# Pool projection moved into the attention loop, and the output projection's first chunk taken by feature blocks

## The reference, cut to what matters

```
def pool_mixer(u, w_pool, pool_scale):
    groups = jnp.split(u, N_POOL, axis=-1)            # 4 groups of 256 features
    outs = [(centred_mean(g, w) - g) @ w_pool[i] for i, (g, w) in enumerate(zip(groups, POOL_WINDOWS))]
    return jnp.concatenate(outs, axis=-1) * pool_scale

mix = jnp.concatenate([context_attention(q, k, v), pool_mixer(u, w_pool[l], pool_scale[l])], axis=-1) @ w_out[l]
yp = yp + m_ctx[2][:, None] * mix                      # the gate row
```

## Time and profile before

| what | value |
|---|---|
| median of 3 runs | 4318.09 us |
| the profiled execution's own time | 4316.63 us |
| its span, first to last instruction | 4315.0 us |
| PE busy | 3882.6 us, 90% |
| DVE, ACT, POOL busy | 2562.3 us, 1821.1 us, 507.7 us |
| mean granted TensorE clock | 0.948 |

### The profile page before, as it was taken

The page is one execution under the profiler, slowest core; times in us unless marked ns, Lnnn a source line. Parts: engine busy times, 40 slices in busy tenths (PEclk is TensorE's granted clock), DMA queues, the critical chain, the costliest instruction groups (busy, mean ns, idle before and its releaser), DMA issues. The chain is left out here.

```text
span 4315.0 us, 69324 instructions
## 1 busy us (share of the span) xinstructions
PE 3882.6 (90%) x25083; PEld 3405.9 (79%) x25083; DVE 2562.3 (59%) x4875; ACT 1821.1 (42%) x2862; POOL 507.7 (12%) x458
## 2 busy tenths in 40 slices
PE   7899999999799997595996299999999999999992
PEld 3688888888688895595995288888888888888881
DVE  4655554555567766231321767777777777777774
ACT  3511111110576663111113066666666666666663
POOL 0000000000444652000000000000000000000000
PEclk9999999999899998798998699999999999999996
DMA  9434434343544445635325167777777777777776
GB/s 350 139 127 134 133 130 137 127 134 116 136 137 113 119 136 195 222 103 176 112 80 190 54 225 253 255 257 258 258 255 255 254 253 254 255 256 254 253 241 251
DMA packets 568508, 818.44 MB, mean 190 GB/s; under 512 B 23600, under 2 KB 455296, under 8 KB 556544
## 3 DMA queue, kind: packets, MB, share of 16 engines
q1 hardware_dynamic: 545760, 699.64, 50.0%
q0 software_dynamic: 22688, 118.02, 8.5%
HBM read 715.89 MB, written 101.71 MB: 189 GB/s over the span
## 5 line engine op out<-in xcount | busy, mean ns | idle before, releaser
L1758 DVE TENSOR_TENSOR e_wlo<-e_raw,e_whi 128x1024 fp32r<-128x1024 f32 x768 | 905.0, 1219 | 355.5 <-ACT e_whi L1674 352.5
L1899 PE MATMUL ps<-e_xs,e_whi 128*128 128x320 f32 x4096 | 1061.4, 345 | 16.6 <-DVE e_xs L1766 9.0
L1899 PE MATMUL ps<-e_xs,e_wlo 128*128 128x160 f32 x4096 | 934.6, 238 | 0.0
L1674 ACT ACTIVATE e_whi<-e_raw 128x1024 fp32r<-128x1024 f32 x768 | 768.9, 1054 | 386.0 <-DMA e_raw<-in_w_gate 153.2
L1899 PEld LDWEIGHTS ps<-e_xs,e_whi 128*128 128x128 f32 x4096 | 754.8, 188 | 26.5 <-DVE e_wlo L1758 13.9
L1899 PEld LDWEIGHTS ps<-e_xs,e_wlo 128*128 128x128 f32 x4096 | 770.1, 191 | 0.7
L1302 PE MATMUL ps<-o_whi,mhi 128*128 128x256 f32 x1280 | 364.5, 285 | 101.2 <-DMA mlo<-mixlo 101.2
L1917 PE MATMUL ps<-e_whi,e_h 128*128 128x512 f32 x1024 | 405.4, 396 | 7.8 <-DVE e_h L1792 7.8
L484 PE MATMUL ps<-hhi,p_whi 128*128 128x512 f32 (+1 forms) x1536 | 386.6, 360 | 8.5 <-DVE p_wlo L423 8.5
L441 DVE SCALAR_TENSOR_TENSOR p_acc<-p_modraw,cT,p_acc 128x256 f32<-128x256 f32 x960 | 386.4, 478 | 0.6 <-DMA p_modraw<-in_w_mod 0.6
L484 PE MATMUL ps<-hlo,p_whi 128*128 128x512 f32 (+1 forms) x1536 | 383.5, 358 | 0.0
(11 more groups left out here) (237 smaller groups left out, 6037.7 us busy)
## 6 DMA issues: line engine op xcount, KB each, us to landing
e_raw<-in_w_gate SPq DMA_DIRECT2D x64, 2048.0 KB
e_raw<-in_w_up SPq DMA_DIRECT2D x64, 2048.0 KB
e_raw<-in_w_down SPq DMA_DIRECT2D x64, 2048.0 KB
p_modraw<-in_w_mod SPq DMA_DIRECT2D x128, 512.0 KB, 3.7
m_raw<-in_w_mod SPq DMA_DIRECT2D x16, 2048.0 KB, 14.6
p_raw<-in_w_in SPq DMA_DIRECT2D x64, 512.0 KB, 4.8
o_raw<-in_w_out SPq DMA_DIRECT2D x16, 2048.0 KB, 8.8
projT<-p_out_st POOLq DMA_DIRECT2D x32, 640.0 KB, 3.6
```

The lines of the kernel that those rows point to most:

```text
L1674: nc.scalar.activation(piece(whi, c, q), piece(raw, c, q), ACT.Copy).then_inc(w_hi_made, 1)
L1758: nc.vector.tensor_tensor(piece(wlo, c, q), piece(raw, c, q), piece(whi, c, q).bitcast(F32), ALU.subtract).then_inc(w_lo_made, 1)
L1899: last = nc.tensor.matmul(bank[:, 0:cols], w[:, s, at:at + P], xs[:, k, 0:cols], start=(k == 0 and w is whi), stop=(k == KD - 1 and w is whi))
```

## The change

In the attention stage:

- `mean_d` is twice as tall and POOL stores each mean block twice, so that output block n finds its pair of input blocks in 256 rows of its own. `w_pool` is copied by 8 DMAs inside DRAM to `wp_d`, laid out by output block.
- In bodies 2 to 7 PE does the projection of block n = j - 2: two fp32 matmuls after `values(5)`, two after `values(7)` and two (of 256 columns) after `values(9)`, all in bank 7. ACT (`pool_high`) reads PSUM, scales and rounds to hi; DVE (`pool_low`) makes lo from PSUM in one operation. Blocks 6 and 7 follow after the loop, one after the other.
- SP at a body's end stores block j - 2 and loads mean, weights and scale of block j - 1.
- The loop over j is written as a loop over 0 and 1 and one over 2 to 7.

In the output projection:

- The first block is gone. The gate rows are made at the start of the second one, in banks 5 to 7.
- SP loads the first weight chunk, then the four quarters of the mix, then the second weight chunk. Each quarter has its own semaphore.
- The first chunk of each half is taken `by_rows`: k outermost, the five tiles inside, in five banks; PE waits for the quarter k // 4 alone. All other chunks go `by_tiles` as before.

So block 7's inputs are asked for only once block 6 is projected and split; block 6's inputs are the last loads of the loop. The core of the diff:

```diff
+            def project_pool(n, t):
+                t0, tn = THIRDS[t]
+                if t == 0:
+                    pe.wait_ge(pool_in, n * 48 + 48)
+                if t:
+                    pe.wait_ge(pooled_lo, n * 3 + (t + AHEAD))
+                for b in range(2):
+                    last = nc.tensor.matmul(pool_bank(t)[:, 0:tn], wpn[:, b, :], mean[:, b, t0:t0 + tn],
+                                            start=(b == 0), stop=(b == 1))
+                last.then_inc(pooled, 1)
...
+            def pool_high(n, t):
+                t0, tn = THIRDS[t]
+                act.wait_ge(pooled, n * 3 + (t + 1))
+                if t == 0:
+                    act.wait_ge(pooled_stored, n * 32 + AHEAD)
+                nc.scalar.activation(plhi[:, t0:t0 + tn], pool_bank(t)[:, 0:tn], ACT.Copy, scale=pscn[:, 0:1]
+                                     ).then_inc(pooled_hi, 1)
...
+            def pool_low(n, t):
+                t0, tn = THIRDS[t]
+                dve.wait_ge(pooled_hi, n * 3 + (t + 1))
+                nc.vector.scalar_tensor_tensor(out=pllo[:, t0:t0 + tn], in0=pool_bank(t)[:, 0:tn], scalar=pscn[:, 0:1],
+                                               in1=plhi[:, t0:t0 + tn].bitcast(F32), op0=ALU.mult, op1=ALU.subtract
+                                               ).then_inc(pooled_lo, 1)
...
+            with pe.Fori(0, 2) as j:
+                body(j, False)
+            with pe.Fori(2, J) as j:
+                body(j, True)
+            pe.wait_ge(batch_read, J * NB + (NB - 1))
+            for n in (NPOOL - 2, NPOOL - 1):
+                for t in range(3):
+                    project_pool(n, t)
...
                 with sp.Fori(0, 2) as g:
                     sp.wait_ge(tile_done, g * (NCH * TPG) + 2 * TPG)
+                    load_w(g, 0, 0)
                     for q in range(4):
                         for dst, src in ((mhi, mixhi_d), (mlo, mixlo_d)):
                             sp.dma_start(dst[:, 4 * q:4 * q + 4, :].bitcast(F32),
                                          src[q * 512:q * 512 + 512, ds(g * GT, GT)].rearrange("(k p) t -> p k t", p=P)
-                                         ).then_inc(mix_in, 16)
-                        if q < 2:
-                            load_w(g, q, q)
+                                         ).then_inc(mix_in[q], 16)
+                    load_w(g, 1, 1)
...
+                def by_rows(g, i, s):
+
+                    for k in range(KD):
+                        if k % 4 == 0:
+                            pe.wait_ge(mix_in[k // 4], g * 32 + 32)
+                            piece_there(g, i, s, k // 4)
+                        for t in range(TPG):
+                            if k == 0:
+                                free_bank(g, i, s, t)
+                            last = products(k, t, s)
+                            if k == KD - 1:
+                                last.then_inc(tile_done, 1)
+                        if k % 4 == 3 and k < KD - 1:
+                            last.then_inc(piece_used, 1)
...
                 with pe.Fori(0, 2) as g:
+                    by_rows(g, 0, 0)
+                    by_tiles(g, 0, 1)
+                    with pe.Fori(1, NCH // 2) as i:
                         for s in range(2):
+                            by_tiles(g, i, s)
```

More of the change, by code:

```diff
@@ L674, in _, with body @@
             load_head(0, 1)
-            with sp.Fori(0, J) as j:
+            for n in range(NPOOL):
+                sp.dma_start(wp_d[n * P:n * P + P], v["wpool"][:, n // 2 * 2:n // 2 * 2 + 2, n % 2 * P:n % 2 * P + P]
+                             ).then_inc(wp_laid, 16)
+            def body(j, pool_load, pool_store):
                 sp.wait_ge(batch_read, j * NB + NB)
@@ L774, in _ @@
                 steps += 2 * PER
[L775 removed]
+            pool.wait_ge(mean_stored, 32 * NPOOL + FIRST)
         @block.scalar
@@ L856, in _, with body @@
             copy_turned(0, 0)
-            with act.Fori(0, J) as j:
+            def body(j, pool):
                 for u in range(U):
@@ L934, in _, with body @@
                 stats(0, u)
-            with dve.Fori(0, J) as j:
+            def body(j, pool):
                 for u in range(U):
@@ L947, in _ @@
                 split_pair(j, W - 1)
+            with dve.Fori(0, 2) as j:
+                body(j, False)
+            with dve.Fori(2, J) as j:
+                body(j, True)
+            for n in (NPOOL - 2, NPOOL - 1):
+                for t in range(3):
+                    pool_low(n, t)
         @block.tensor
@@ L1032, in _, with body @@
             turn(0, 0)
-            with pe.Fori(0, J) as j:
+            def body(j, pool):
                 for u in range(U):
@@ L1074, in output_projection @@
     with nc.sbuf_tensor("gate_row", [P, 2, D], F32) as gate_row:
[L1075 to L1157, removed]
-                    for t, (t0, tn) in enumerate(THIRDS):
-                        dve.wait_ge(pooled_hi, 3 * n + t + 1)
-                        nc.vector.tensor_tensor(pllo[:, n % 2, t0:t0 + tn], pl[:, n % 2, t0:t0 + tn],
-                                                plhi[:, n % 2, t0:t0 + tn].bitcast(F32), ALU.subtract
-                                                ).then_inc(pooled_lo, 1)
@@ L1287, in _ @@
             def _(pe):
+                for c in range(2):
+                    for b in range(4):
+                        n = 4 * c + b
+                        if n >= 8 - TPG:
+                            pe.wait_ge(gate_read, n - (8 - TPG) + 1)
+                        for k in range(4):
+                            col = modT[:, 32 + 4 * b + k, c:c + 1].broadcast_to([P, P])
+                            last = nc.tensor.matmul(ps[:, gate_bank(n), k * P:k * P + P], col, ident[:],
+                                                    start=True, stop=True)
+                        last.then_inc(gate_turned, 1)
@@ new lines, in products, with free_bank @@
+                def products(k, t, s):
+                    wh, wl = (w[:, s, k * CW:k * CW + CW] for w in (whi, wlo))
+                    mh, ml = (m[:, k, t * P:t * P + P] for m in (mhi, mlo))
+                    for j, (m, w) in enumerate(((mh, wh), (mh, wl), (ml, wh))):
+                        last = nc.tensor.matmul(ps[:, t, 0:CW], m, w, start=(k == 0 and j == 0),
+                                                stop=(k == KD - 1 and j == 2))
+                    return last
+                def free_bank(g, i, s, t):
+                    pe.wait_ge(gated, g * (NCH * TPG) + i * (2 * TPG) + (s * TPG + t + 1))
@@ new lines, in by_tiles @@
+                def by_tiles(g, i, s):
+                    for t in range(TPG):
+                        free_bank(g, i, s, t)
+                        for k in range(KD):
+                            if t == 0 and k % 4 == 0:
+                                piece_there(g, i, s, k // 4)
+                            last = products(k, t, s)
+                            if t == TPG - 1 and k % 4 == 3 and k < KD - 1:
+                                last.then_inc(piece_used, 1)
+                        last.then_inc(tile_done, 1)
```

112 lines of the change are left out of this document (76 added, 36 removed).

## The result

The changed kernel takes 4281.74 us, median of 4 runs (4267.68 to 4289.08), beside 4316.04 us for the kernel before; the ratio is 0.9923, 95% interval 0.991 to 0.9935. Run again on another occasion (`e0_again`) it was 4275.76 us, ratio 0.9912 (0.9895 to 0.9928). So the change makes the kernel 34 to 39 us faster, where -30.6 us was forecast.

A forecast was written before the change was run, and what follows sets the result against it. PE was taken to bound attention, with idle stretches of 64.5, 45.9 and 47.7 us open to gain. Terms 25.8 - 9 - 47.4 = -30.6 us on 4316.6 gave 4286.0, forecast as 4287 us, range 4264 to 4306.

The forecast's parts named there:

- Part 1: Pool matmuls moved into attention bodies 2 to 7: nothing hides their 4.3 us per body, +25.8 us.
- rival C: Pool work half hidden in PE's stalls, or the tail at full clock: 4274 or 4278, together 4265 us; chance 0.17.
- Rival A: Attention bodies lose their clock as PE waits for DVE's lo: +48 us, 4335 us; chance 0.07.
- Part 2: Pool stage of 64.5 us replaced by a tail of 55.3 us for blocks 6 and 7, at clock 0.5: -9 us.
- the bounds given: For the tail: 46 us at the full clock, -18 us; with everything 5 us later, -4 us.
- Part 3: Output projection's two starts: chunk 0 runs beside the loads, each half's chunk 1 starts 23.7 us earlier, together -47.4 us.
- the new wait: Between chunk 0 and chunk 1, PE waits 1.9 us for DVE's lo of chunk 1.
- the 0.70 of the earlier trace: Clock in the second 4 us of dense matmuls, then 1.00; cited for taking clock 0.5 in the tail.
- three quarters late by 2 us each: Bound on the gain at the starts: with each quarter 2 us later than PE, -33 us.
- Rivals B and D: Chunk 0 at half clock, +53 us, 4340 us, chance 0.03; quarters landing together near the end, 4314 us, chance 0.05.

The follow-up runs named there:

- e5_half_pool: The changed kernel without the second of each two pool projection matmuls, so half the input features are missing: 4258.29 us, ratio 0.987 against the kernel before.
- e1_pool_only: The changed kernel's attention stage and tail, with the old load order and one wait for all quarters: 4326.3 us against 4314.91 for the kernel before, ratio 1.0031.
- after: The changed kernel itself, set against the kernel before: 4281.74 us, ratio 0.9923; its profiled execution spans 4266.1 us.
- e2_starts_only: The kernel before with its pool stage kept, only the new load order and each half's first chunk by feature blocks: 4262.11 us, ratio 0.9876.
- e6_tail: The changed kernel with block 6's loads issued mid-body, block 7 reusing its mean, and pieces alternating between two banks: 4242.91 us, ratio 0.9834 against the kernel before.
- e4_all_rows: The changed kernel with every chunk of the output projection by feature blocks over five tiles: 4375.35 us, ratio 1.0145 against the kernel before.

## Why the prediction was right, point by point

**Forecast and range.** 4287 us was forecast, 4281.74 measured, inside 4264 to 4306; -30.6 us forecast, -34 and -39 measured.

**Part 1, bodies 2 to 7, +25.8 us.** Right in mechanism, slightly low in size. PE bounds the bodies, and each microsecond of matmul adds about one, which `e5_half_pool` shows from the other side. Over the nine profiles with the new attention stage and full matmuls the six bodies take 423.6 to 430.4 us, mean 428.3, against 400.8 and 401.1 in the two with the old one: +27.4 us, 4.6 per body where 4.3 was set. The stall of the second head stayed whole, so rival C's hiding did not happen. Rival A, the bodies that lose their clock, did not either: PE's waits for DVE's lo are 1.8 us in all, longest 0.3, far below the 2 us from which it was to decide.

**Part 2, the tail, -9 us.** The steps hold; the clock is the term that was mis-sized. 55.3 us were set, with both blocks at 0.5 and 14 us each. With the blocks mostly at 0.5 the tail is 54.3 us (`e1_pool_only`); in `after`, where the clock rose after the first piece of each, the blocks took 10.9 and 11.0 us and the tail 49.7 us. Rival C's other half, the tail at the full clock (46 us), so came true in part. Of the bounds given, 46 and 60, both values lie inside. The loads were 13.0 us to block 6's start (12.5 set) and, for block 7, 9.4 us from the end of block 6 to its first matmul (9.3 set).

**Part 3, the starts, -47.4 us.** 48.3 us measured, and 47.4 to 48.7 in the four other profiles with these starts (`e0_again`, `e2_starts_only`, `e5_half_pool`, `e6_tail`). Each term held: first matmul at 19.4 us (20.3 set), chunk 0 in 31.4 us (31.2 set), the new wait 1.7 us (1.9 set). Two slips in the working changed nothing: the 0.70 of the earlier trace rows is a window that begins 2.7 us behind the first matmul, not the second 4 us, and three quarters late by 2 us each would leave -35 of the gain, not -33. Rivals B and D (slow chunk 0; quarters that don't stream) are out by the clock and by the lack of any wait inside chunk 0.

**What was missed.** The forecast priced the pool part as +25.8 - 9, so as a loss of 17 us, which `e1_pool_only` confirms in sign (+11.4 us), but I forecast the whole change and did not ask for the part that pays: the starts alone are 14 us faster than the full change (`e2_starts_only`). Nor did I look at what could be had from the tail. With its inputs asked for in time, a second bank and tiles of its own for block 7, the same split gives 33 us more. Some of the closeness is luck: the errors of the bodies (+1.6 us against their average) and of the tail (-6 us) have opposite signs, and the code that nobody touched moves by more than either of them between executions. And in `e4_all_rows` I took a boundary of chunks by rows for the one by tiles.

## What to carry to other kernels

Moving matmuls from their own stage into one that PE already bounds gained nothing here by itself: look at what the old stage spent on waits, and make sure that what is left behind (here the last two of eight blocks) doesn't spend it again on loads that could have been issued earlier. Where a stage begins with a large load, take the reduction dimension as the outer loop over as many accumulators as PSUM holds, give each piece its own semaphore, and order the queue by first use; then change back to the old loop, since at the end all accumulators come due together. A step's price moves with what is next to it: the same loop order that gave some 18 us at each half's start cost 7 us at each inner boundary.

## What the runs showed of the hardware

- Bodies of one attention loop, with the same instructions, differed with the share of time at the two TensorE clock levels: four of 71.3 to 71.6 us at a mean granted clock of 0.93, then 69.5 us at 0.98 and 68.2 us at 0.97 (`after`). In the body of 69.5 us PE was busy 2.2 us less than in the one before it, which is all of the difference.
- Three matmuls per bank and then another bank (`e4_all_rows`) ran as fast as 48 in one bank: 0.12 us per matmul at clock 1.00 in both.
- The jump back of a loop of 1440 written matmuls on PE, with the DMA engines full (share 1.01), left PE idle for 4.36 and 4.31 us in two profiles, and no such gap stood there once the loop was written out. The loop of attention shows 0.2 us at its jumps.
